# Spreading 144 vector products differently over a two-block transformer kernel, and moving two of six shift rounds from ScalarE to VectorE

## The reference

```python
mod = c_act @ w_ada + b_ada                       # c_act = silu(c), one row of 2048
shift, scale, gate = jnp.split(mod, 3, axis=-1)
h = rms_norm(x, g) * (1.0 + scale[:, None]) + shift[:, None]
proj = jnp.einsum('bsd,df->bsf', h, w_in)         # then attention heads and retention heads
y = jnp.concatenate([y_a * silu(z_a), y_r * silu(z_r)], axis=-1)
x = x + gate[:, None] * (y @ w_out)               # rms_norm, then the second block:
# layer 1: differential attention, 8 heads of 2 score maps; layer 2: forgetting attention, 16 heads
# each: h = x * (1 + scale) + shift; y = attention(h); x = layer_norm(alpha * x + gate * y, g, b)
```

## Time and profile before

| | |
|---|---|
| median of three runs | 1496.9 us (1496.42 to 1496.92) |
| the profiled execution | 1496.42 us, span 1494.6 us |
| PE busy | 1427.5 us, 96% of the span |
| DVE busy | 1169.1 us, 78% |
| ACT busy | 722.5 us, 48% |
| POOL busy | 117.9 us, 8% |
| read from HBM | 445.65 MB, 300 GB/s over the span |
| mean granted TensorE clock | 0.992 |

### The profile page before, as it was taken

One profiled execution on the slowest core, in us unless ns is written; L12 is line 12 of the kernel. 1 busy time (PEld: TensorE's weight loads), 2 busy tenths in 40 slices (PEclk: granted clock), 3 DMA queues, 4 the chain that ended last, 5 costly groups with the idle time before them and its releaser, 6 DMA issues.

```text
span 1494.6 us, 19097 instructions
## 1 busy us (share of the span) xinstructions
PE 1427.5 (96%) x6634; PEld 1177.8 (79%) x6634; DVE 1169.1 (78%) x1458; ACT 722.5 (48%) x1034; POOL 117.9 (8%) x217
## 2 busy tenths in 40 slices
PE   4799999999999899999999999989999999999996
PEld 3677777887887688888887878878888888888885
DVE  5999898877999799898667659878697865556566
ACT  4464554554434634444556644464345544455431
POOL 1111001001000001010010100000010000000000
PEclk9999999999999999999999999999999999999998
DMA  9999999877999599999867679759698786555762
GB/s 389 414 412 413 392 359 394 287 264 244 385 416 347 191 407 383 412 384 381 309 214 252 188 269 364 262 192 356 244 385 300 252 282 207 178 179 155 266 194 89
DMA packets 99870, 448.85 MB, mean 300 GB/s; under 512 B 11424, under 2 KB 13776, under 8 KB 76496
## 3 DMA queue, kind: packets, MB, share of 16 engines
q1 hardware_dynamic: 69840, 249.33, 46.9%
q0 software_dynamic: 26352, 185.63, 31.8%
q10 hardware_dynamic: 3600, 12.85, 2.2%
HBM read 445.65 MB, written 2.12 MB: 300 GB/s over the span
## 4 chain that ended last, share of the span: by engine, by line
PE 76%; DVE 14%; issue 3%; ACT 3%; DMA 3%; SPq 0%; POOL 0%; DVEq 0%; ACTq 0%
PE bank L741 22%; PE bank L743 22%; PE bank L742 22%; DVE gw L1425 6%; DVE w_lo L1417 4%; PE bank L951 2%; PE bank L899 2%; DMA gw<-in_t_ada 1%; PE bank L716 1%; PE bank L908 1%; DMA raw<-in_t_steps 1%; DVE area L1425 1%; ACT probs L1081 1%; PE bank L927 1%; PE bank L881 1%
## 5 line engine op out<-in xcount | busy, mean ns | idle before, releaser
L1022 ACT CAST w_hi<-raw 128x1024 fp32r<-128x1024 f32 x448 | 468.7, 1050 | 647.5 <-PE bank L743 544.4
L1405 DVE TENSOR_TENSOR w_lo<-raw,w_hi 128x1024 fp32r<-128x1024 f32 x372 | 451.4, 1223 | 260.4 <-ACT w_hi L1022 259.5
L741 PE MATMUL bank<-w_hi,act_hi 128*128 128x512 f32 x1504 | 601.3, 400 | 3.1 <-DVE w_lo L1405 3.1
L742 PE MATMUL bank<-w_lo,act_hi 128*128 128x512 f32 x1536 | 598.7, 390 | 0.0
L743 PE MATMUL bank<-w_hi,act_lo 128*128 128x512 f32 x1504 | 587.5, 391 | 0.0
L1425 DVE CUSTOM_DVE_ANT_0 gw<-gw,c_act 128x2048 f32<-128x2048 f32 x170 | 388.1, 2285 | 4.0 <-DMA gw<-in_t_ada 4.0
L742 PEld LDWEIGHTS bank<-w_lo,act_hi 128*128 128x128 f32 x1536 | 289.1, 188 | 57.2
L741 PEld LDWEIGHTS bank<-w_hi,act_hi 128*128 128x128 f32 x1504 | 282.9, 188 | 61.0 <-issue 3.6
L743 PEld LDWEIGHTS bank<-w_hi,act_lo 128*128 128x128 f32 x1504 | 282.6, 188 | 60.7
L1417 DVE TENSOR_TENSOR w_lo<-raw,w_hi 128x1024 fp32r<-128x1024 f32 x84 | 101.6, 1220 | 15.3 <-ACT w_hi L1022 15.1
L585 POOL DMA_DIRECT2D gw<-in_t_mod x96 | 51.6, 537 | 729.3 <-DVE products L1425 723.1
(11 more groups left out here) (174 smaller groups left out, 1003.3 us busy)
## 6 DMA issues: line engine op xcount, KB each, us to landing
raw<-in_t_steps SPq DMA_DIRECT2D x464, 512.0 KB, 5.7
gw<-in_t_mod POOLq DMA_DIRECT2D x96, 1024.0 KB, 7.7
gw<-in_t_ada POOLq DMA_DIRECT2D x42, 1024.0 KB, 8.3
gw<-in_t_kv_mod POOLq DMA_DIRECT2D x32, 1024.0 KB, 8.0
area<-in_t_ada POOLq DMA_DIRECT2D x6, 1024.0 KB, 10.7
area<-gate_rows ACTq DMA_DIRECT2D x3, 1024.0 KB, 12.9
area<-in_ln_g ACTq DMA_DIRECT2D x2, 1024.0 KB, 6.1
area<-in_ln_b ACTq DMA_DIRECT2D x2, 1024.0 KB, 9.2
```

Of the source, the lines that this page charges most:

```text
L741: nc.tensor.matmul(dst, hi, w[:, k], start=(kt == 0), stop=False)
L742: nc.tensor.matmul(dst, hi, w_lo[:, j % SLOTS, k], start=False, stop=False)
L1022: nc.scalar.copy(w_hi[:, b], raw[:, j % SLOTS]).then_inc(hi_ready, 1)
L1405: nc.vector.tensor_tensor(w_lo[:, j % SLOTS], raw[:, j % SLOTS], w_hi[:, j % LEAD].bitcast(F32), ALU.subtract).then_inc(lo_ready, 1)
```

## The change

It has three parts. (1) The table of GEMVs has other numbers: fewer in pairs 2, 3, 9 to 15 and 17, more in pairs 4, 5, 6, 18, 19, 20 (4 before, 8 now) and 22, with other bounds in pairs 2 to 5. The sum stays 144. (2) Tile rounds 4 and 6 of both norms are shifted by DVE instead of ACT, and the splits of halves 6 and 7 of the next pair stand together behind round 7. (3) `silu(c_2)` is taken by ACT in half 1 of pair 5 instead of half 9 of pair 4, so its call moves from the first loop to `pair`.

```diff
-PAIR_TILES = {2: 3, 3: 9, 4: 6, 5: 8, 6: 9, 7: 8, 8: 5, 9: 8, 10: 8, 11: 8, 12: 8, 13: 8, 14: 4, 15: 4, 16: 3, 17: 5,
-              18: 3, 19: 6, 20: 4, 21: 8, 22: 3, 23: 5, 24: 4, 25: 4, 26: 3}
+PAIR_TILES = {2: 2, 3: 7, 4: 7, 5: 9, 6: 10, 7: 8, 8: 5, 9: 7, 10: 7, 11: 7, 12: 7, 13: 7, 14: 3, 15: 3, 16: 3, 17: 4,
+              18: 5, 19: 7, 20: 8, 21: 8, 22: 4, 23: 5, 24: 4, 25: 4, 26: 3}
...
-BY_ACT = (1, 3, 4, 5, 6, 7)
-BY_DVE = (0, 2)
+BY_ACT = (1, 3, 5, 7)
+BY_DVE = (0, 2, 4, 6)
...
-DECAYS_AT, LAMBDA_AT, C_AT = (3, 1), (3, 4), (4, 9)
+DECAYS_AT, LAMBDA_AT, C_AT = (3, 1), (3, 4), (5, 1)
...
-    if pair == 4:
-        return [(h, first + i) for i, h in enumerate((0, 1, 3, 4, 12, 14))]
-    begin, end = {2: (9, 16), 3: (0, 16), 5: (0, 15), 8: (1, 9), 18: (1, 9), 22: (0, 7)}.get(pair, (1, 14))
+    begin, end = {2: (10, 16), 4: (1, 12), 5: (4, 16), 8: (1, 9), 18: (1, 9), 22: (0, 7)}.get(pair, (1, 14))
...
+                    if static and (p0, h) == C_AT:
+                        silu_of_c(2)
...
-                    if at == C_AT:
-                        silu_of_c(2)
...
                 low_round(3)
                 chunk = 2 * p0 + 2
                 chunk_halves(0, 2, chunk, (4,))
+                shift_round(4)
                 low_round(4)
                 low_round(5)
                 chunk_halves(0, 2, chunk, (5,))
+                shift_round(6)
                 low_round(6)
-                chunk_halves(0, 2, chunk, (6,))
                 low_round(7)
-                chunk_halves(0, 2, chunk, (7,))
+                chunk_halves(0, 2, chunk, (6, 7))
```

## The result

| | before | changed |
|---|---|---|
| median of the timed runs | 1496.91 us (4 runs) | 1507.57 us (4 runs, 1506.67 to 1507.67) |
| ratio to before | | 1.0073, 95% interval 1.006 to 1.0085 |
| profiled execution | 1496.42 us, span 1494.6 | 1511.03 us, span 1509.2 |
| mean granted TensorE clock | 0.992 | 0.986 |

The kernel is 10.7 us slower; 6.7 were forecast, and 1507.6 lies 0.8 above the range. The direction was right. The profiled execution is itself 3.5 us above the median. Of that, 2.0 us lie in pairs 0 to 2, of which the change touches only the end (a product fewer from half 9 of pair 2 on, where the profile is already 2.4 us behind): against the profile of before this part varies from -0.5 to +2.0 between the kernels profiled here, also where its instructions are the same. I leave it out of the account.

A forecast was written before the change was run, and what follows sets the result against it. PE, busy 96% of the span, was taken as the bound, with changes only where it waits; the terms -0.8 -0.6 +0.9 +0.2 -0.9 +1.7 +2.9 +3.3 sum to +6.7 on 1496.42, so 1503.1 us, range 1499.2 to 1506.8.

The forecast's parts named there:

- rival three: PE's clock falls to 1.2 GHz behind two new stalls, 1 to 2 us each, giving 1506; chance 0.14.
- Other pairs: Pairs without their own term: GEMVs lost or gained where the lead is over 2 us cost 0.
- The front: Pair 3, halves 57 to 65: old waits for DVE's split shrink, a new 1.1 us stall at half 57; -0.8 us.
- Pair 4: A GEMV in front of a maximum moves away, ending PE's 0.58 us wait for ACT: -0.6 us.
- pair 15: The GEMV of half 7 that held a maximum is gone, with ACT's 0.88 us wait: -0.9 us.
- both norms: DVE's added shifts lengthen its chain and stall PE at halves behind each norm: +1.7 us first, +2.9 second.
- Half 335: In pair 20, 8 GEMVs for 4 use up DVE's lead and PE stalls for the split: +3.3 us.
- Rival two: Pair 20: DVE's lead is refilled ahead of half 10, its 3.3 us term is 0, time 1499.8; chance 0.10.
- inert: Whole kernel: unseen lead covers the added stalls, within 0.2% of 1496.9, up to 1499.9; chance 0.03.
- The product of half 14 in pair 5: This GEMV comes ahead of POOL's inverse root of a retention head, whose load waits for an earlier GEMV: +0.2 us.
- 0.9 in pair 5: A GEMV between half 6's split and the maximum delays ACT's exponential, for which PE already waits: +0.9 us.

The follow-up runs named there:

- e10: Kernel before with 8 vector products in pair 20 and 7 in each of pairs 10 to 13, forget matmuls not moved: 1502.24 us against 1497.80, ratio 1.0026.
- e9: Kernel before with 8 vector products in pair 20, 7 in pairs 10 to 13, and the 48 forget matmuls in front of half 335: 1497.34 us against 1497.80.
- e8: The changed kernel run and profiled again, no edit: 1507.23 us against 1496.92 for the kernel before, ratio 1.0064.
- e5: The changed kernel with the 48 forget matmuls put in front of half 335: 1504.23 us against 1507.23 for the changed kernel.
- e6: The changed kernel with pair 5's nine vector products moved to halves 4, 5, 7 and 9 to 14: 1509.39 us, ratio 1.0082 to the kernel before.
- e1: Kernel before with only the new product numbers of pairs 2 to 6 and the moved silu: 1498.47 us against 1497.62, ratio 1.0007.
- e2: Kernel before with only tile rounds 4 and 6 shifted by DVE and the split of half 6 behind round 7: 1502.69 us against 1497.62, ratio 1.0035.
- e3: Kernel before with 8 vector products in pair 20 instead of 4 and 7 in each of pairs 10 to 13: 1501.41 us against 1497.62, ratio 1.0028.
- e4: Kernel before with 7 vector products in pair 20 and 7 in each of pairs 11 to 13: 1499.67 us, ratio 1.0013.
- e12: Kernel before with products redistributed over pairs 2 to 7, 15, 17, 18, those of pairs 9 and 19 later, silu in pair 5: 1491.33 us against 1497.80.

## Why the prediction was off

**The step that failed is the price of the waits: the clock stood at 0 in the sum, and rival three had too small a chance.** The prediction priced every new wait at its own length and gave "the clock" 0.14, with 1 to 2 us for each fall, and only "if two of them bring the clock down". The row of the second norm, idle for 1.97 us and then at 0.50, was read against the row of the first norm, 3.60 us of idle time and no fall. I took the two as a contradiction that left little of the rule. The runs show that both are outcomes of the same thing: behind the 2.3 us in pair 5 the clock fell in two profiles of four, behind 2.9 to 3.0 in four of five, ahead of the first norm in 10 of 14. One profile could not tell this. So a wait of 3.1 us should have been entered with its expected fall. The full fall costs 12 matmuls x 0.2 = 2.4 us and 0.3 in the small matmuls behind, 2.7 in the first profile. Over the five profiles that have the wait the mean is 1.8 (2.7, 2.8, 1.7, 1.7, 0.1), and e10 against e9 gives 1.8 too, though against the kernel before it is 0.7 to 1.3. In pair 5 half of 1.6 is 0.8. With 1.8 + 0.8 the forecast would have been 1505.7.

**A term put at nothing.** "Other pairs lose or gain GEMVs where the lead is over 2 us and no row beside them shows a PE wait: 0" covered pair 18, which went from three products to five. PE's idle time ahead of the second norm grew with it, and half 0 of pair 19 started 0.4, 1.5, 1.3 and 0.5 us later in the four profiles (changed, e8, e5, e6), 0.9 on average. The lead over PE's matmuls was the wrong thing to look at there: what waits is PE's first transpose, for DVE's norm chain. With this 0.9 and the 0.45 below, the terms add up to 10.65, against 10.7 measured. That they meet so well is luck in part, since the clock's share alone is known to no better than 1 us. The parts measured by themselves (e1 0.8, e2 5.1, e3 3.8) add up to 9.7.

The Trainium skill ("TensorE: Matmul & The Clock Gate", "What's actually happening") says that idleness throttles the clock, which the filled hole of e5 and e9 bears out.

**What held.** The front: the new wait at half 57, forecast at 1.1, is this row, and the two that were to shrink gave 1.6 back.

```profile
204.82 0.50 PE L700 MATMUL bank<-w_hi,act_hi 128*128 128x512 f32 x1 [1.06 <-DVE w_lo L1415]
```

Pair 4 and pair 15 gave what they were to give, within 0.2. From half 2 on both norms came within 0.1 of the sum, and at the first wait by wait: 1.55, 1.26 and 0.54 at halves 6, 8 and 9 were forecast from start to start, and the rows have idle times of 1.30, 0.97 and 0.29, each with some 0.2 more in starts.

```profile
518.00 0.47 PE L739 MATMUL bank<-w_hi,act_hi 128*128 128x512 f32 x1 [1.30 <-DVE w_lo L1403]
524.69 0.47 PE L739 MATMUL bank<-w_hi,act_hi 128*128 128x512 f32 x1 [0.97 <-DVE w_lo L1403]
527.95 0.50 PE L739 MATMUL bank<-w_hi,act_hi 128*128 128x512 f32 x1 [0.29 <-DVE w_lo L1403]
```

Four shifts on DVE took 1.36 us, as the earlier trace rows said, so the shorter time that the prediction estimated from the Trainium skill ("VectorE: DVE Perf Modes", section "The TRN2 errata") is not what this trace has. Half 335 waited 3.1 for 3.3. Rival two is out with it, and so is "inert".

**A term mis-sized.** The product of half 14 in pair 5, ahead of POOL's inverse root, was entered at 0.2 and cost 0.65 in both profiles. The wait for the retention head's `area` is new:

```profile
348.68 1.96 PE L949 MATMUL bank<-area,probs 128*128 128x256 f32 x8 [0.41 <-DVE area L1852]
```

Its bound was 0.8; the reason for the low value ("DVE is not behind there") looked at the wrong engine. POOL's load waited for the GEMV until 345.14, its inverse root began only at 346.02, and DVE waited 0.62 us for that.

## What to carry to other kernels

Where an engine's lead over its consumer is what counts, the lead at each place (end of the producer, start of the consumer) can be added and subtracted like a balance, and it forecast eight waits here to within 0.3 us (0.9 in pair 5, 1.1 at half 57, four at the first norm, 3.3 at half 335 and 1.1 in e4). Every wait of TensorE that is long enough (here 2 us and more) should be entered twice, at its length and with a share of what the next dozen matmuls cost at half clock; filling it with work that is ready anyway saves both (e9 against e10). Work that can float, such as these products, belongs where the lead is large and away from the last chain that a consumer is waiting for: moving those behind each norm by a few halves gave 3.3 us by the trace and 4.3 timed, while taking more of them into a full pair gave the gain back. And one profile shows one outcome: where two rows of it seem to contradict each other, the same row in a second profile is worth more than an argument.

## What the runs showed of the hardware that was not expected

The granted clock behind the same wait of the same instructions is not the same in every execution: 1.00 or 0.76 (over 7 us) behind 2.3 us in pair 5, 0.50 or 1.00 behind 2.9 us in pair 20, 1.00 or 0.56 (over 3 us) behind 3.6 us at the first norm. Whether this makes the executions of a kernel scatter is not shown: e6 spans 1503.93 to 1513.34 in 6 runs, but e12, whose profile has such a fall too, 1490.68 to 1492.76 in 5. And around 420 us ACT's casts wait for the loads of the weights in the kernel before as in e12 (0.85 and 2.04 us for the same cast), so a gain on TensorE in front of it can be lost to a wait there, as in e6 and e12, and need not be, as in e8.
